# Attention steps: a step's probability transposes ahead of the scores of the step two on

## What is computed

```
qkv = hn @ w_qkv                          # 16 query heads, 4 key/value heads, head width 64
q, k = rmsnorm(q) * 64 ** -0.5, rmsnorm(k)
s_band = q_chunk . k_band - slope * dist  # each chunk of 64 queries sees 128 keys: its own and the chunk before
s_meta = q_chunk . k_meta                 # and the 16 meta keys
probs = softmax([s_meta, s_band, sink])[..., :-1]
out = probs_meta . v_meta + probs_band . v_band
return out @ w_o
```

## Time and profile before

| | |
|---|---|
| median of 3 runs | 1878.55 us |
| the profiled execution | 1878.34 us |
| its span, first to last instruction | 1876.5 us |
| mean granted TensorE clock | 0.999 of full speed |
| TensorE busy | 1867.1 us (99%) |
| VectorE busy | 959.9 us (51%) |
| ScalarE busy | 598.4 us (32%) |
| GpSimd busy | 350.1 us (19%) |

### The profile page before, as it was taken

One profiled execution on the slowest core, in us unless ns is written; L12 is line 12 of the kernel. 1 busy time (PEld: TensorE's weight loads), 2 busy tenths in 40 slices (PEclk: granted clock), 3 DMA queues, 4 the chain that ended last, 5 costly groups with the idle time before them and its releaser, 6 DMA issues.

```text
span 1876.5 us, 33932 instructions
## 1 busy us (share of the span) xinstructions
PE 1867.1 (99%) x13919; PEld 1767.1 (94%) x13919; DVE 959.9 (51%) x1083; ACT 598.4 (32%) x702; POOL 350.1 (19%) x629
## 2 busy tenths in 40 slices
PE   9999999999999999999999999999999999999999
PEld 8999999999999999999999999999988788888887
DVE  6443356668865443344564443445557654434443
ACT  5222222332243222222342222223456442222232
POOL 2888889315230000000000000000012000000000
PEclk9999999999999999999999999999999999999999
DMA  6322544447423332332243223322321233333322
GB/s 184 90 84 84 155 135 130 162 140 191 118 73 89 94 89 86 110 90 73 71 126 90 84 84 101 90 81 80 115 62 46 66 93 94 90 96 101 111 70 87
DMA packets 330785, 188.29 MB, mean 100 GB/s; under 512 B 8152, under 2 KB 323832, under 8 KB 330712
## 3 DMA queue, kind: packets, MB, share of 16 engines
q1 hardware_dynamic: 323216, 166.71, 30.0%
q0 software_dynamic: 7088, 20.38, 3.9%
q10 hardware_dynamic: 408, 0.17, 0.0%
HBM read 174.91 MB, written 11.14 MB: 99 GB/s over the span
## 4 chain that ended last, share of the span: by engine, by line
PE 96%; DVE 2%; issue 1%; ACT 1%; POOL 0%; POOLq 0%; DVEq 0%
PE ps L807 79%; PE ps L1048 5%; PE ps L1159 2%; PE ps L1090 2%; PE ps L1109 1%; PE ps L1298 1%; PE ps L1260 1%; PE ps L1200 0%; PE ps L1009 0%; PE ps L1008 0%; PE ps L999 0%; DVE r L1621 0%; PE ps L1221 0%; PE ps L1211 0%; ACT xh L1321 0%
## 5 line engine op out<-in xcount | busy, mean ns | idle before, releaser
L807 PE MATMUL ps<-xh,wh 128*128 128x264 f32 (+1 forms) x2432 | 557.7, 299 | 0.3 <-DVE t_a L1653 0.2
L807 PE MATMUL ps<-xh,wl 128*128 128x264 f32 (+1 forms) x2432 | 556.6, 299 | 0.0
L807 PE MATMUL ps<-xl,wh 128*128 128x264 f32 (+1 forms) x2432 | 556.6, 299 | 0.0
L1591 DVE TENSOR_TENSOR wl<-raw,wh 128x2048 fp32r<-128x2048 f32 x171 | 400.2, 2340 | 168.4 <-ACT wh L1309 168.4
L1309 ACT ACTIVATE wh<-raw 128x2048 fp32r<-128x2048 f32 x172 | 327.6, 1905 | 246.4 <-PE ps L807 205.5
L807 PEld LDWEIGHTS ps<-xh,wh 128*128 128x128 f32 x2432 | 385.4, 188 | 15.1 <-issue 1.5
L807 PEld LDWEIGHTS ps<-xl,wh 128*128 128x128 f32 x2432 | 385.2, 188 | 13.8 <-issue 0.2
L807 PEld LDWEIGHTS ps<-xh,wl 128*128 128x128 f32 x2432 | 385.2, 188 | 13.8
L807 PE MATMUL ps<-act_h,wh 128*128 128x264 f32 (+1 forms) x1232 | 282.2, 299 | 0.0
L807 PE MATMUL ps<-act_h,wl 128*128 128x264 f32 (+1 forms) x1232 | 281.7, 299 | 0.0
L807 PE MATMUL ps<-act_l,wh 128*128 128x264 f32 (+1 forms) x1232 | 281.6, 298 | 0.0
(11 more groups left out here) (313 smaller groups left out, 1685.9 us busy)
## 6 DMA issues: line engine op xcount, KB each, us to landing
raw<-in_ff_w_gate SPq DMA_DIRECT2D x88, 512.0 KB, 3.7
raw<-in_ff_w_up SPq DMA_DIRECT2D x87, 512.0 KB, 4.7
raw<-in_ff_w_down SPq DMA_DIRECT2D x64, 384.0 KB, 3.8
raw<-in_ff_w_down SPq DMA_DIRECT2D x64, 320.0 KB, 3.5
raw<-in_even_w_in SPq DMA_DIRECT2D x16, 512.0 KB, 4.8
raw<-in_attn_w_qkv SPq DMA_DIRECT2D x12, 512.0 KB, 4.5
raw<-in_even_w_out SPq DMA_DIRECT2D x8, 512.0 KB, 4.3
raw<-in_attn_w_o SPq DMA_DIRECT2D x8, 512.0 KB, 4.4
```

The source lines that it names most:

```text
L807: last = nc.tensor.matmul(ps[:, 2 * pair + hf, 0:nh], w[:, slot, b * P:(b + 1) * P], x[:, k0 + k, c0 + hf * nh:c0 + (hf + 1) * nh], start= ...
L1591: v.tensor_tensor(wl[:, c % 2, :], raw[:, c % 2, :], wh[:, c % 2, :].bitcast(F32), ALU.subtract).then_inc(wl_ready, 1)
```

## The change

Pass n of TensorE's loop now runs meta_values(n-1), the fill, probs_t(n), and then scores(n+2), the cover and values(n). Everything else, the lists of the other engines among it, is as before.

```
@@ -1267,13 +1267,13 @@
             for n in range(NB):
                 g, j = divmod(n, NT)
-                if n + 2 < NB:
-                    scores(n + 2)
                 if n:
                     meta_values(n - 1)
                 for d, k0, k1 in fill.get(n, ()):
                     out_part(d, k0, k1)
                 probs_t(n)
+                if n + 2 < NB:
+                    scores(n + 2)
                 sums = g + 1 if j == 0 and g + 1 < NKV else None
                 if g + 2 < NKV:
                     query_part(g + 2, j // 2, j % 2, sums)
```

## The result

The changed kernel takes 1890.38 us (median of 6 runs, 1887.89 to 1892.99) beside 1878.32 us for the kernel before: a ratio of 1.0066, 95% interval 1.0056 to 1.0076, or about 12 us more. The direction was as forecast. The size is more than twice the 5.5 us of the forecast, and 1890.38 us lies above its range of 1882.0 to 1887.6.

What follows compares the result with a forecast made beforehand. TensorE was taken to bound the kernel, carrying 96% of its chain. Terms of 1.0 (step 0), 1.7 (step 9), 3.35 (steps 10 to 13) and -0.55 gave 5.5 us: 1884.0 us as a median, range 1882.0 to 1887.6.

Steps and rivals of the forecast that it cites:

- The ring: Attention steps: scores, softmax, normed, transposes and next scores wait on each other in turn, 5.1 us between softmax starts.
- The gap at step 0: Step 0: TensorE stands idle until normed(0) is done, +1.0 us.
- The values of step 13: Leaving the attention steps: values(13) start 1.66 us behind softmax(15), formerly 2.20, bound by out_low; -0.55 us.
- The wait for GpSimd: Scores of step 12: TensorE's 1.3 us wait for the norm of group 3 vanishes into the later start.
- Rivals 2 and 3: Whole kernel: no loss, 1877.5 to 1878.6 us, chance 0.08; only part of the loss, 1880.5 to 1882.3 us, chance 0.07.
- Steps 1 to 8: nothing: Steps 1 to 8: the query part covers the wait for normed with 0.3 us left over, so no loss.
- Its own signs of being wrong: Attention steps: softmax starts still about 4 us apart, query-part steps above 5.4 us, or a granted clock of 0.5.
- Steps 10 to 13: Steps 10 to 13: four turns of 5.1 us, 0.1 us more for fills, 20.5 us against 17.15; +3.35 us.
- softmax(11): Step 9: its start comes 2.7 us late, 1.0 from step 0 and 1.7 from groups now before scores(11).
- No row shows..., bounded: Steps 10 to 13: turn latency lies between 5.0 and 5.35 us, 0.4 us less or 1.0 us more in four turns.
- the upper end of its case: Whole kernel: top of the main estimate, with slower turns and 0.8 us lost in steps 1 to 8; 1885.9 us.
- Rival 1: Steps 10 to 13: idle gaps lower TensorE's clock; one fall 1885.4 us, three turns low some 1889; chance 0.2.

Runs made afterwards that it cites:

- a1: The changed kernel run again with nothing altered; median 1890.84 us (1889.21 to 1893.94).
- d2: New order in steps 9 to 13 alone, VectorE there running copy of the transposes, softmax, out_low, normed, reduce; median 1882.06 us.
- d1: The changed kernel with its TensorE gaps in steps 9 to 13 filled by products nobody needs; median 1887.95 us (1887.60 to 1889.70).
- a4: Kernel before, its order kept, with one query-part block put between scores and meta values in six steps; median 1880.61 us.
- b1: New order in steps 9 to 13 alone, with VectorE's normed moved ahead of the reduce there; median 1893.54 us.
- a2: Kernel before with the new order in steps 1 to 8 alone; median 1880.74 us (1880.29 to 1882.60).
- d3: Kernel before with scores moved behind the meta values only, ahead of fill and transposes, in every step; median 1879.14 us.

## Why the prediction was wrong

**Direction and mechanism: right.** The ring through scores, softmax, normed and transposes is in the chain of waits, and VectorE's edits show that its waits cost time. The gap at step 0 is 0.93 us (1.0 forecast). The values of step 13 stand 1.67 us behind softmax(15), 0.53 us closer than before (0.55 forecast). The wait for GpSimd is gone without any gain, and nothing behind the steps changed but 0.2 us. Rivals 2 and 3, no loss and only a part of it, fall.

**"Steps 1 to 8: nothing": the step that failed.** It was priced by rows in which each group had its old neighbour. Transposes ahead of a query part cost 0.52 us, ahead of scores 0.70; scores ahead of meta values 0.92, ahead of a query part 1.02. That is +0.3 us in each of steps 0 to 8, 2.7 us that the forecast put at nothing, and it is no wait, so comparing arrival times with `pn_ready` could not show it. The sign of it stood in the earlier trace rows: at step 0 scores took 1.02 us before the transposes, at step 1 0.92 before the meta values. The prediction read the 0.1 us as time filled until normed came. Its own signs of being wrong appeared: query-part steps longer than 5.4 us (5.69), and in a1 a granted clock of 0.5 in the stretch.

**"Steps 10 to 13", the ring of 5.1 us: mis-sized, by the same term and by a wait for the copy.** Transposes in it cost 0.69 us, not 0.52; the two turns without a fill took 5.28 and 5.22 us. With a fill the prediction let the values' wait for out_low set the pace, 3.48 us from softmax to transposes. Measured are 3.67: the meta values wait for the copy L2029 and start 0.77 us behind the values, not 0.59, which the prediction had no term for; d2, with the copy early, has 0.59 and turns with a fill 0.18 us shorter. Transposes behind the fill cost 0.64 us, and the turn is 5.44. Four turns: 21.4 for 20.5 us, +4.25 against 17.15, not +3.35. softmax(11) was 5.5 us later behind softmax(1) than before, not 2.7: 2.7 from the switches of nine steps, 0.2 from those of step 9.

**"No row shows..., bounded": the bound from above was too low.** It let the transposes cost 0.7 us but for another reason, in the ring alone, and never in steps 1 to 8. With the measured terms the sum is 0.93 + 1.7 + 2.9 + 4.25 - 0.53 = 9.2 us, as measured to the values of step 13; the profiled execution is 9.55 us longer. The prediction's arithmetic holds but for small sums: the upper end of its case comes to 1885.8 by its own terms, not 1885.9, and two falls at 1.4 us above 1884.0 to 1886.8, not 1887.6.

**Rival 1, the clock, 0.2: it happened, beside the sum and not in its place.** d1 against the changed kernel prices it at 2.4 to 2.9 us in the median. It was held to be a rival although it adds to the main case. Its price of 1.4 us a fall was read a little low: from the start of the first of the eight products to the start of the ninth are 3.50 us (1379.48 to 1382.98), and at 0.23 us each they would take 1.84, so about 1.7 us. And it fitted one fall, where a1 had one three times as long, for 3.6 us. The argument against it, that no fall followed the 1.34 us gap, was luck of that profile: in a4 one did. 9.5 and 2.5 us make the 12 measured.

## What to carry to other kernels

Price a moved group of matmuls by its new neighbours, not by the row at its old place: start-to-start spacings hold only for the pair they were read on, and groups that contract over 64 partitions belong side by side. When the producer of a wait is fed by the instructions that stood ahead of it, moving them behind it makes a ring; add up one full turn, and look at every wait of the engine in that turn, those of its weight loads too, since moving one operation to the front pushes another (here the copy of b1) into the ring. And where a change puts small gaps into every step of a stretch, add the cost of a lower TensorE clock to the sum and look at several executions, for one profile may miss it.

## What was not expected of the hardware

A change between products over 64 and over 128 partitions costs TensorE about 0.3 us there and back, with no wait that the profile names: the trace of it is the spacing of starts (a2, +0.3 us a step; a4, +0.33; d3, with the same neighbours, nothing). In a1 TensorE's clock fell behind gaps of at most about 0.9 us each (busy 1.12 and 1.43 of 2 us in the last two stretches ahead of the fall), and useless products in the gaps kept it up: all five executions of d1 have a mean clock of 0.999 or more, with a median of 1887.95 us, 1890.38 and 1890.84 without them.
